# Three reorderings in a two-block transformer kernel: top-k rounds over four partition quadrants, expert pieces loaded one program sooner, feed-forward loads issued in another order

## The chip, the cores and the metric

The kernel runs on one core of a Trainium2 chip. Its time is the device time of one execution in microseconds (us), as the median of repeated runs. A core has a tensor engine (PE, with its weight loads as PEld), a vector engine (DVE), a scalar engine (ACT), GpSimd (POOL), and a sync engine (SP) whose queue issues nearly all DMAs here.

## The reference, cut to what matters

Sequence 1024, width 1024, float32. Two layers of a first block, then one second block:

```python
for l in range(DEPTH):                      # DEPTH = 2
    mod = einsum('bd,dk->bk', silu(c), w_ada[l]) + b_ada[l]     # six vectors of 1024
    h = rms_norm(x, norm1_g[l]) * (1.0 + scale1) + shift1
    ...                                     # attention and a 31 tap convolution, mixed by w_out
    x = x + gate1 * mix
    h2 = rms_norm(x, norm2_g[l]) * (1.0 + scale2) + shift2
    x = x + gate2 * expert_choice_ffn(h2, w_router[l], w_gate[l], w_up[l], w_down[l])
# expert_choice_ffn: 16 experts, each takes the 128 tokens with the largest affinity
    aff = softmax(einsum('bsd,de->bse', h, w_router))
    gate, idx = top_k(aff.transpose(0, 2, 1), 128)
    xe = h[idx]; hid = silu(xe @ w_gate) * (xe @ w_up); ye = (hid @ w_down) * gate
# second block: hgrn2 and rg-lru, then
    gate, up = split(hn @ w_gate_up); h = h + (silu(gate) * up) @ w_down
```

## The kernel before, in words

Each stage is a program of its own (an `nc.Block`): every engine has a list of instructions, they meet through semaphores, and no engine begins the next program before all have ended the last. Float32 products are made of high and low parts: ACT writes `hi`, DVE writes `lo`, and PE runs three matmuls for each product. One body of code serves both layers, so a line stands in the trace once for each.

**`conv_norm_and_mix`** ends with the w_out product. At its end SP loads rows of `w_ada` into the rows 0 to 3 of the tile `mix`; rows 4 to 7 and the weight tile `first_w` are no longer read by then. Its last instruction on DVE is the sum at L1517.

**`route`** is the next program. It (1) makes `h` (the normed tokens) and the router's logits and softmax; (2) chooses on DVE, for each of 16 experts and each half of the tokens, the 128 largest of 512 affinities: 32 rows of 512 on partitions 0 to 31, 16 rounds of `max` (the next eight values, L1720), `max_index` (their places, L1721) and `match_replace` (the eight struck out, L1722), each waiting for the one before; (3) on PE turns the eight blocks of `h` (L1774), which ACT copies to `rt_rows` (L1685) and SP stores to `h2_rows` (L1659, `h_rows` in the trace), 512 KB each; (4) on PE, between the blocks, adds up 16 products (`mod_row_step`, L1747) for the next layer's modulation. Each takes one 512 KB row of `w_ada` from a ring of four buffers `rt_ada` (SP, L1648). When all 16 are done, ACT copies the sums (L1689, semaphore `row_taken`), and PE turns them (L1788). PE's list has the wait for `row_taken` ahead of L1781 and L1782, which turn the chosen places and values back for the slot computation (L1725 to L1735 on DVE). SP also loads the first six 1 MB pieces of expert weights here (L1796), two ahead of the `rt_ada` ring and four behind its first four rows. ACT's list casts pieces 0 and 1 (L1679) ahead of the first copy of a block.

**`run_experts`** follows. Its first instruction on POOL gathers the rows of expert 0 from `h2_rows`, and PE waits for them.

**`mix_and_feed_forward`** is the last program. It runs in units: `FFT` = 22 units of gate and up, then four chunks of four units of down (units 22 to 37). A unit is seven products of PE (L3022), i = 0 to 6. SP loads a unit's raw weights with `load_raw(n)` (768 KB for unit 23 on), one of two buffers (`first_w`, `ff_raw`). Chunk 0 reads seven blocks of hidden values, 1.5 MB each, back from DRAM into slots (`load_slot`, tiles `ff_near` and `ff_rest`, L2917); `store_block` writes such blocks (L2901), `load_x` brings the rows of x back (L2922). POOL makes the sums of a unit's weights (L2996), ACT and DVE split them, and DVE does the split of unit n + 1's first sums ahead of the evacuation of unit n (L3299) that PE's product i = 4 of unit n waits for.

All loads and stores named here are in SP's one queue, in the order of SP's list.

Of the kernel before, what the change touches and what calls it, by code (L numbers as in the profile page):

```python
# [21 lines left out]
P = 128  # L22
S = 1024
# [33 lines left out]
SPLIT_EARLY = 2  # L57
N_MOD = 6
# [71 lines left out]
def build(nc, A):  # L130
# [3 lines left out]
    with ExitStack() as top:  # L134
# [397 lines left out]
        def layer(l):  # L532
            with ExitStack() as ctx:
# [8 lines left out]
                gate = (modl[:, 2, :], modl[:, 5, :])  # L542
                with ExitStack() as mixing:
                    mixing.enter_context(own_semaphores())
                    mix = sb("mix", [P, DT, S], F32, mixing)
# [22 lines left out]
                    conv_norm_and_mix(l, lc, mix, gate[0], modl)  # L568
                with own_semaphores():
                    experts_part(l, lc, modl, gain, shift[1], gate[1])  # L570
# [753 lines left out]
        def conv_norm_and_mix(l, lc, mix, gate, modl):  # L1324


            with ExitStack() as ctx:
# [11 lines left out]
                w_in = [sem(f"lo_w_in{b}") for b in range(LO_BUFS)]  # L1339

# [20 lines left out]
                with nc.Block() as block:  # L1361
                    @block.sync
                    def _(sp):
# [25 lines left out]
                        load_ada(LATE_RING + ends[1], n_steps)  # L1389

# [176 lines left out]
        def experts_part(l, lc, modl, gain, shift, gate):  # L1567
            with ExitStack() as ctx:
# [3 lines left out]
                with ExitStack() as running:  # L1572
                    raw = [sb(f"ex_raw{i}", [P, 4, HALF], F32, running)[:] for i in range(RAW - 1)]
# [17 lines left out]
        def route(l, lc, modl, gain, shift, slots, slot_gate, token, pieces):  # L1591
# [3 lines left out]
            with ExitStack() as ctx:  # L1595
# [15 lines left out]
                aff_t = sq_sum[0:2 * EXPERTS, 0:HALF]  # L1611
                best, place, place_f = (sq_sum[0:2 * EXPERTS, HALF + n * CAP:HALF + (n + 1) * CAP] for n in range(3))
                place = place.bitcast(U32)
                chosen = sb("chosen", [P, 2, 2, EXPERTS], F32, ctx)
# [13 lines left out]
                mod_bank, cols_bank, back_psum = 5, 1, psum[:, 5, 0:4 * EXPERTS]  # L1628
# [10 lines left out]
                with nc.Block() as block:  # L1639
                    @block.sync  # L1640
                    def _(sp):
# [23 lines left out]
                    def _(act):  # L1665
# [10 lines left out]
                        act.copy(aff_t, bank(0)[0:2 * EXPERTS, :]).then_inc(aff_copied, 1)  # L1676
# [15 lines left out]
                    def _(dve):  # L1692
# [2011 lines left out]
```

## Time and profile before

| | |
|---|---|
| median of 3 runs | 3468.09 us (3467.51 to 3471.37) |
| profiled execution | 3468.38 us, span 3466.6 us |
| PE busy | 3278.0 us, 95% of the span |
| DVE busy | 2723.0 us, 79% |
| DMA | 708.43 MB, mean 204 GB/s |

The profiled execution lies 0.3 us over the median. Busy time is summed over stages with different limits, so the idle stretches of PE, and what ends each, say more than the share.

### The profile page before, as it was taken

The numbers are of one execution on the slowest core, as the hardware profiler recorded it, in microseconds if no ns is written. First come the engines' busy times: TensorE is split into PE (matmuls) and PEld (weight loads), VectorE is DVE, ScalarE is ACT, GpSimd is POOL, SyncE is SP. The second block draws the span as 40 slices with busy tenths as digits, with TensorE's granted clock in tenths as the row PEclk, the third lists the DMA queues.
The fourth block names the chain that finished last, engine by engine and source line by source line (L and its number), as shares of the span: only waits on it lengthen the run. The fifth ranks groups of instructions, "written<-read, shape, count | busy, mean of one in ns | idle before, by whom it ended". The sixth has DMA issues, their size and how long they took to land. (4 is left out here: it accounts for less than half of the span.)

```text
span 3466.6 us, 43873 instructions
## 1 busy us (share of the span) xinstructions
PE 3278.0 (95%) x15396; PEld 2599.7 (75%) x15396; DVE 2723.0 (79%) x2529; ACT 1812.3 (52%) x1933; POOL 683.4 (20%) x530
## 2 busy tenths in 40 slices
PE   6999997999999899999889999999999999999898
PEld 3847973788888686597558888887877778888686
DVE  6987777898989789778789898985844498888667
ACT  5244543788888633445258888863242353344223
POOL 0202200111111020220011111103444032333232
PEclk9999998999999999999999999999999999999999
DMA  5110057999999411003689999972110334444863
GB/s 194 37 67 20 8 194 261 360 393 400 390 398 392 182 49 70 19 12 133 238 315 401 389 403 389 400 294 91 52 43 13 129 109 161 143 159 140 340 252 134
DMA packets 144682, 708.43 MB, mean 204 GB/s; under 512 B 19248, under 2 KB 27952, under 8 KB 91824
## 3 DMA queue, kind: packets, MB, share of 16 engines
q1 hardware_dynamic: 133392, 669.89, 50.4%
q0 software_dynamic: 8928, 32.51, 3.5%
q10 hardware_dynamic: 2240, 4.46, 0.3%
q8 instruction: 70, 1.15, 0.1%
q14 instruction: 52, 0.43, 0.0%
HBM read 617.14 MB, written 85.46 MB: 203 GB/s over the span
## 5 line engine op out<-in xcount | busy, mean ns | idle before, releaser
L2070 DVE TENSOR_TENSOR ex_lo<-ex_raw,ex_hi 128x2048 fp32r<-128x2048 f32 x320 | 727.4, 2290 | 114.0 <-ACT ex_hi L2004 111.3
L2004 ACT CAST ex_hi<-ex_raw 128x2048 fp32r<-128x2048 f32 x316 | 604.9, 1915 | 123.3 <-PE psum L1926 116.7
L1924 PE MATMUL psum<-ex_hi,xe_hi 128*128 128x512 f32 x1024 | 403.1, 394 | 1.3 <-DVE xe_lo L2075 1.3
L1926 PE MATMUL psum<-ex_hi,xe_lo 128*128 128x512 f32 x1024 | 400.0, 391 | 0.0
L1925 PE MATMUL psum<-ex_lo,xe_hi 128*128 128x512 f32 x1024 | 400.0, 391 | 0.0
L583 DVE SCALAR_TENSOR_TENSOR mix<-y,lcols,mix 128x1024 f32<-128x1024 f32 x186 | 274.3, 1477 | 6.0
L3022 PE MATMUL psum<-ff_rest,w_hi 128*128 128x512 f32 x776 | 241.2, 392 | 15.7 <-DVE ff_ev L3299 9.8
L1924 PEld LDWEIGHTS psum<-ex_hi,xe_hi 128*128 128x128 f32 x1024 | 193.3, 189 | 41.1 <-issue 2.0
L1926 PEld LDWEIGHTS psum<-ex_hi,xe_lo 128*128 128x128 f32 x1024 | 193.1, 189 | 40.5
L1925 PEld LDWEIGHTS psum<-ex_lo,xe_hi 128*128 128x128 f32 x1024 | 193.2, 189 | 38.9
L1924 PE MATMUL psum<-ex_hi,hid_hi 128*128 128x512 f32 x512 | 205.2, 401 | 0.0
L1926 PE MATMUL psum<-ex_hi,hid_lo 128*128 128x512 f32 x512 | 200.3, 391 | 0.0
L1925 PE MATMUL psum<-ex_lo,hid_hi 128*128 128x512 f32 x512 | 199.4, 390 | 0.0
L1873 POOL COPY idx_in<-slots 128x1 uint32 (+1 forms) x32 | 14.4, 451 | 900.5 <-PE psum L1910 516.2
L3022 PEld LDWEIGHTS psum<-ff_rest,w_hi 128*128 128x128 f32 x776 | 145.6, 189 | 49.6 <-issue 12.9
L1223 ACT ACTIVATE y<-psum,neg_max,q_scale 128x1024 f32<-128x1024 f32 x64 | 77.3, 1207 | 165.2 <-DVE neg_max L1264 165.2
L3022 PE MATMUL psum<-ff_rest,ff_a_hi 128*128 128x512 f32 x512 | 158.9, 392 | 2.8 <-DVE ff_rest L3438 1.5
L3022 PE MATMUL psum<-ff_rest,w_lo 128*128 128x512 f32 x388 | 151.8, 391 | 0.0
L2070 DVE TENSOR_TENSOR ex_lo<-first_w,ex_hi 128x2048 fp32r<-128x2048 f32 x64 | 146.5, 2288 | 3.0 <-ACT ex_hi L2004 3.0
L478 PE MATMUL psum<-h_hi,in_hi 128*128 128x512 f32 x384 | 123.1, 402 | 26.2 <-DVE h_lo L694 23.1
L2004 ACT CAST ex_hi<-first_w 128x2048 fp32r<-128x2048 f32 x64 | 121.8, 1903 | 25.7 <-PE psum L1926 25.7
L478 PE MATMUL psum<-xn_hi,w_hi 128*128 128x512 f32 x384 | 120.9, 396 | 7.2 <-DVE xn_lo L2171 6.7
(524 smaller groups left out, 7458.5 us busy)
## 6 DMA issues: line engine op xcount, KB each, us to landing
ex_raw<-w_experts_dram SPq DMA_DIRECT2D x320, 1024.0 KB, 7.3
first_w<-w_experts_dram SPq DMA_DIRECT2D x64, 1024.0 KB, 7.9
hid_rows<-x SPq DMA_DIRECT2D x71, 512.0 KB, 3.7
mix<-w_ada_dram SPq DMA_DIRECT2D x64, 512.0 KB, 4.6
first_w<-w_in_dram SPq DMA_DIRECT2D x42, 512.0 KB, 3.5
ff_rest<-hid_rows SPq DMA_DIRECT2D x13, 1536.0 KB, 14.5
rt_ada<-w_ada_dram SPq DMA_DIRECT2D x32, 512.0 KB, 7.9
ff_raw<-w_gate_up_dram SPq DMA_DIRECT2D x11, 1024.0 KB, 7.8
```

The lines of the kernel that those rows point to most:

```text
L478: mm = pe.matmul(bank(out + half), wt, xt[:, half * HALF:(half + 1) * HALF], start=first and n == 0, stop=last and n == 2)
L583: dve.scalar_tensor_tensor(out=acc, in0=y[:, j, t:t + S], scalar=lc("conv_w")[:, j * TAPS_PAD + t:j * TAPS_PAD + t + 1], in1=acc, op0=ALU. ...
L1223: act.activation(probs[:, slot, :], score_slot(slot), ACT.Exp, bias=neg_max[:, slot:slot + 1], scale=q["q_scale"][:, h, blk], accum_out=ro ...
L1873: pool.tensor_copy(idx_in[:], slots[:, bass.ds(e, 1)]).then_inc(idx_in_done, 1)
L1924: pe.matmul(bank(out), x_hi, h[:, k, :], start=first, stop=False)
L1925: pe.matmul(bank(out), x_hi, r[:, k, :], start=False, stop=False)
L1926: mm = pe.matmul(bank(out), x_lo, h[:, k, :], start=False, stop=end)
L2004: act.copy(hi[j % PARTS][:], raw[j % RAW][:]).then_inc(w_hi, 1)
L2070: dve.tensor_tensor(lo[j % PARTS][:], raw[j % RAW][:], hi[j % PARTS][:].bitcast(F32), ALU.subtract).then_inc(w_lo, 1)
L3022: mm = pe.matmul(out, wt[:, k, :], xt(k), start=fresh and k == 0 and j == 0, stop=k == kt - 1 and j == 2, skip_group_check=True)
```

## The change

1. **Rounds over quadrants.** The affinities of round r lie in the partitions of quadrant r % 4 (32 partitions each). `match_replace` reads quadrant r % 4 and writes the next one, so each quadrant keeps the state in which its eight values were found. `max_index` runs once in four rounds, over all 128 partitions, and the last `match_replace` is left out. Afterwards the values and places of the four quadrants are put in one row again: four copies of 32x32 on DVE (places), four on POOL (values).
2. **Order on PE.** L1781 and L1782 (turning the choice back) write bank 0 rather than 5, and the wait for `row_taken` stands behind the flip matmul.
3. **Three pieces sooner.** Pieces 0, 1 and 5 of the first expert (1 MB each) are loaded at the end of `conv_norm_and_mix`, into `mix` rows 4 to 7 and `first_w`; that program's SP waits until they have landed. `mix` is kept for the whole layer and serves as raw buffers 0 to 3.
4. **Feed-forward loads.** `load_raw(23)` moves behind slots 0 and 1; `load_raw(25)` moves from behind the wait for `late_out` and the loads of slots 7 and 8 to right behind `load_x(3)`.

```diff
+WITH_MIX = (0, 1, RAW - 1)
...
+                mix = sb("mix", [P, DT, S], F32, ctx)
+                raw = [mix[:, row:row + 2, :].rearrange("p a (b n) -> p (a b) n", n=HALF) for row in (HEADS, HEADS + 2, 0, 2)]
...
                         load_ada(LATE_RING + ends[1], n_steps)
+                        sp.wait_ge(lo_done, DT)
+                        sp.wait_ge(lo_split, DT)
+                        for j in WITH_MIX:
+                            load_piece(sp, early_raw[j], 0, j).then_inc(pieces_in, 16)
+                        sp.wait_ge(pieces_in, 16 * len(WITH_MIX))
...
-                        for j in range(SPLIT_EARLY):
-                            load_piece(sp, raw[j], 0, j).then_inc(loaded[j], 16)
+                        for j in WITH_MIX:
+                            sp.sem_inc(loaded[j], 16)
                         load_ada(0, NEXT_RING)
-                        for j in range(SPLIT_EARLY, RAW):
-                            load_piece(sp, raw[j], 0, j).then_inc(loaded[j], 16)
+                        for j in range(RAW):
+                            if j not in WITH_MIX:
+                                load_piece(sp, raw[j], 0, j).then_inc(loaded[j], 16)
...
                         for r in range(CAP // 8):
-                            at = slice(8 * r, 8 * r + 8)
-                            ch.step(dve.max(best[:, at], aff_t))
-                            ch.step(dve.max_index(place[:, at], best[:, at], aff_t))
-                            ch.step(dve.match_replace(aff_t, best[:, at], aff_t, -1.0))
-                        dve.tensor_copy(place_f, place).then_inc(place_done, 1)
+                            q, at = quadrant(r % 4), slice(r // 4 * 8, r // 4 * 8 + 8)
+                            ch.step(dve.max(best[q, at], states[q, :]))
+                            if r % 4 == 3:
+                                ch.step(dve.max_index(place[:, at], best[:, at], states))
+                            if r + 1 < CAP // 8:
+                                ch.step(dve.match_replace(states[quadrant((r + 1) % 4), :], best[q, at], states[q, :], -1.0))
+                        for q in range(4):
+                            dve.tensor_copy(place_row[:, in_row(q)], place[quadrant(q), :]).then_inc(place_done, 1)
...
+                    @block.gpsimd
+                    def _(pool):
+                        for q in range(4):
+                            pool.wait_ge(step, best_steps(CAP // 8 - 4 + q))
+                            pool.tensor_copy(best_row[:, in_row(q)], best[quadrant(q), :]).then_inc(best_copied, 1)
...
-                        pe.wait_ge(row_taken, 4)
-                        pe.wait_ge(place_done, 1)
+                        pe.wait_ge(place_done, 4)
+                        pe.wait_ge(best_copied, 4)
...
+                        pe.wait_ge(row_taken, 4)
                         for j in range(DT // 2):
...
                         n = FFT - 1
                         late = period_blocks(n)
-                        load_raw(n + 2)
                         stored(n_products * DOWN_CHUNKS[0] - 1)
                         for m, i in enumerate((0, 1, 2, 3, 4, 4, 5)):
                             load_slot(m, n, i)
+                            if m == 1:
+                                load_raw(n + 2)
...
                         load_x(3)
+                        load_raw(FFT + 3)
                         sp.wait_ge(late_out, 16 * LATE_BLOCKS)
                         for m in range(n_products, SLOTS):
                             load_slot(m, n, 6)
-                        for n in range(FFT + 1, n_units):
+                        for n in range(FFT + 2, n_units):
```

**SP's list where `conv_norm_and_mix` ends and `route` begins.** The line numbers are those of each kernel; `mix` from `w_ada_dram` is the last modulation row of the ending program, an `UNCONDITIONAL_BRANCH` is the change of program. Before:

```order
L1377 DMA mix<-w_ada_dram 128x1024
L1361 UNCONDITIONAL_BRANCH
L1640 UNCONDITIONAL_BRANCH
L1642 ISA
L1642 DMA w_r<-w_router_dram 128x8x16
L1796 ISA
L1796 DMA ex_raw<-w_experts_dram 128x2048
```

And now:

```order
L1384 DMA mix<-w_ada_dram 128x1024
L1832 ISA
L1832 DMA mix<-w_experts_dram 128x2048
L1832 ISA
L1832 DMA mix<-w_experts_dram 128x2048
L1832 ISA
L1832 DMA first_w<-w_experts_dram 128x2048
L1368 UNCONDITIONAL_BRANCH
L1665 UNCONDITIONAL_BRANCH
L1667 ISA
L1667 DMA w_r<-w_router_dram 128x8x16
```

Three pieces have moved ahead of the change of program, and the ring of `rt_ada` comes first in `route`.

**SP's list in the feed-forward, from the raw weights of unit 22 (`first_w`) on.** `ff_raw` from `w_down_dram` is unit 23 at first and unit 25 the second time; `ff_near` and `ff_rest` from `hid_rows` are slots, `x` from `x_rows` is `load_x`. Before:

```order
L2896 DMA ff_raw<-w_down_dram 128x1536
L2917 DMA ff_near<-hid_rows 128x3072 x2
L2917 DMA ff_rest<-hid_rows 128x3072 x5
L2901 DMA hid_rows<-x 128x1024 x3
L2896 DMA first_w<-w_down_dram 128x1536
L2901 DMA hid_rows<-ff_near 128x1024 x2
L2922 DMA x<-x_rows 128x2x1024
L2901 DMA hid_rows<-ff_rest 128x1024 x4
L2922 DMA x<-x_rows 128x2x1024 x2
L2917 DMA ff_rest<-hid_rows 128x3072
L2917 DMA ff_near<-hid_rows 128x2048
L2917 DMA ff_rest<-hid_rows 128x1024
```

And now:

```order
L2953 DMA ff_near<-hid_rows 128x3072 x2
L2932 DMA ff_raw<-w_down_dram 128x1536
L2953 DMA ff_rest<-hid_rows 128x3072 x5
...
L2958 DMA x<-x_rows 128x2x1024 x2
L2932 DMA ff_raw<-w_down_dram 128x1536
L2953 DMA ff_rest<-hid_rows 128x3072
L2953 DMA ff_near<-hid_rows 128x2048
L2953 DMA ff_rest<-hid_rows 128x1024
```

Unit 23's weights went behind two slots, and unit 25's (before, the row after the twelve shown) ahead of the last three slot loads.

## Rows read from the trace of the kernel before

**Rows 1.** The page: busy us, share and instructions of each engine.

```profile
PE 3278.0 (95%) x15396; PEld 2599.7 (75%) x15396; DVE 2723.0 (79%) x2529; ACT 1812.3 (52%) x1933; POOL 683.4 (20%) x530
```

**Rows 2.** Waits of layer 1's `route`, 545 to 616 us: total, times, longest.

```profile
PE psum L1747 <- DMA rt_ada<-w_ada_dram: 10.5, 5, 7.0
...
PE psum L1781 <- ACT rt_ada L1689: 3.4, 1, 3.4
```

**Rows 3.** DVE in order of time: start, us, line, tiles, idle before.

```profile
564.33 0.68 DVE L1720 MAX8 sq_sum<-sq_sum 32x8 f32<-32x512 f32 x1 [1.31 <-ACT sq_sum L1676]
565.05 0.08 DVE L1721 MATCH_VALUE_LOAD sq_sum<-sq_sum 32x8 f32 x1
...
565.83 0.08 DVE L1722 MATCH_VALUE_LOAD sq_sum<-sq_sum 32x8 f32 x1
...
566.61 0.68 DVE L1720 MAX8 sq_sum<-sq_sum 32x8 f32<-32x512 f32 x1
...
600.75 0.21 DVE L1723 CAST sq_sum<-sq_sum 32x128 f32<-32x128 uint32 x1
...
605.25 0.17 DVE L1737 TENSOR_TENSOR mod<-psum,b_ada 128x16 f32<-128x16 f32 x1
```

**Rows 4.** PE in order of time, the products of the modulation.

```profile
574.43 3.58 PE L1747 MATMUL psum<-rt_ada,c_act 128*1 128x512 f32 x8 [7.04 <-DMA rt_ada<-w_ada_dram]
...
597.17 1.03 PE L1747 MATMUL psum<-rt_ada,c_act 128*1 128x512 f32 x4 [0.24 <-DMA rt_ada<-w_ada_dram]
```

**Rows 5.** ACT in order of time, the first two block copies and `row_taken`.

```profile
567.81 1.90 ACT L1685 COPY rt_rows<-psum 128x1024 f32<-128x1024 f32 x2
...
600.16 2.37 ACT L1689 COPY rt_ada<-psum 1x512 f32<-1x512 f32 x4
```

**Rows 6.** Windows of `route`: busy by engine, then TensorE clock, DMA share, GB/s.

```profile
550.00:574.00 24.00, 15.86 (x72) 4.92 (x72) 18.41 (x35) 15.22 (x15) 0.00 (x0) 0.86 1.01 406
574.00:597.00 23.00, 19.30 (x84) 6.73 (x84) 21.93 (x53) 5.06 (x5) 0.00 (x0) 0.82 0.94 347
```

**Rows 7.** SP's last issue in `conv_norm_and_mix` of layer 1.

```profile
534.53 0.33 SPq L1377 DMA_DIRECT2D mix<-w_ada_dram  x1
```

**Rows 8.** DVE's last instruction in that program.

```profile
546.18 0.18 DVE L1517 TENSOR_TENSOR modl<-psum,b_ada 128x24 f32<-128x24 f32 x1 [4.47 <-PE psum L217]
```

**Rows 9.** Waits of PE in the feed-forward, 3180 to 3300 us.

```profile
PE psum L3022 <- DVE ff_ev L3299: 9.1, 2, 7.2
...
PE psum L3022 <- DMA ff_rest<-hid_rows: 5.5, 4, 2.4
```

**Rows 10.** SP's issues in the feed-forward.

```profile
3204.03 0.33 SPq L2896 DMA_DIRECT2D ff_raw<-w_down_dram  x1
...
3242.80 1.40 SPq L2922 DMA_DIRECT2D x<-x_rows  x2
3251.74 0.33 SPq L2917 DMA_DIRECT2D ff_rest<-hid_rows  x1
...
3253.06 0.43 SPq L2896 DMA_DIRECT2D ff_raw<-w_down_dram  x1
```

**Rows 11.** PE in the feed-forward: product 1 of unit 21, products of units 24, 25.

```profile
3200.81 0.62 PE L3022 MATMUL psum<-ff_near,ff_a_hi 128*128 128x512 f32 x2
...
3269.94 1.19 PE L3022 MATMUL psum<-ff_rest,w_hi 128*128 128x512 f32 x2 [7.24 <-DVE ff_ev L3299]
...
3278.80 0.61 PE L3022 MATMUL psum<-ff_near,w_hi 128*128 128x512 f32 x2
```

**Rows 12.** POOL: the first sums of unit 25.

```profile
3266.12 0.99 POOL L2996 TENSOR_TENSOR ff_s<-ff_raw 128x384 f32<-128x384 f32 x1 [12.53 <-DMA ff_raw<-w_down_dram]
```

**Rows 13.** DVE: the last weight split of unit 23.

```profile
3239.12 0.96 DVE L3289 TENSOR_TENSOR w_lo<-ff_raw,w_hi 128x768 fp32r<-128x768 f32 x1 [0.23 <-ACT w_hi L3087]
```

**Rows 14.** Windows of the feed-forward, columns as in rows 6.

```profile
3206.00:3264.00 58.00, 49.36 (x212) 39.04 (x210) 35.34 (x50) 14.98 (x25) 11.99 (x10) 1.00 1.01 417
3268.00:3274.00 6.00, 4.06 (x10) 3.22 (x11) 4.33 (x7) 1.24 (x2) 1.77 (x3) 0.50 0.01 3
```

More of the change, by code:

```diff
@@ L542, in layer @@
                 gate = (modl[:, 2, :], modl[:, 5, :])
+                mix = sb("mix", [P, DT, S], F32, ctx)
+                assert CT == HEADS == 4
+                raw = [mix[:, row:row + 2, :].rearrange("p a (b n) -> p (a b) n", n=HALF) for row in (HEADS, HEADS + 2, 0, 2)]
                 with ExitStack() as mixing:
                     mixing.enter_context(own_semaphores())
-                    mix = sb("mix", [P, DT, S], F32, mixing)
                     with ExitStack() as before:
@@ L567, in layer @@
                         attend(l, lc, y, mix, q)
-                    conv_norm_and_mix(l, lc, mix, gate[0], modl)
+                    conv_norm_and_mix(l, lc, mix, gate[0], modl, raw)
                 with own_semaphores():
-                    experts_part(l, lc, modl, gain, shift[1], gate[1])
+                    experts_part(l, lc, modl, gain, shift[1], gate[1], raw)
         def conv_taps(dve, lc, y, mix, step, done):
@@ L1322, in _, with conv_norm_and_mix @@
                                                      op0=ALU.mult, op1=ALU.add).then_inc(centred, 1)
-        def conv_norm_and_mix(l, lc, mix, gate, modl):
+        def conv_norm_and_mix(l, lc, mix, gate, modl, pieces_raw):
             with ExitStack() as ctx:
@@ L1339, in conv_norm_and_mix @@
                 w_in = [sem(f"lo_w_in{b}") for b in range(LO_BUFS)]
+                pieces_in = sem("lo_pieces_in")
+                load_piece = expert_pieces(l)
+                early_raw = {j: pieces_raw[j] for j in WITH_MIX[:-1]}
+                early_raw[RAW - 1] = first_w[:].rearrange("p b k m -> p (b k m)").rearrange("p (a n) -> p a n", n=HALF)
                 def raw_of(n):
@@ L1565, in _, with experts_part @@
                         inverse_norms(act, r, sum_bank, sq_sum)
-        def experts_part(l, lc, modl, gain, shift, gate):
+        def experts_part(l, lc, modl, gain, shift, gate, raw):
             with ExitStack() as ctx:
@@ L1572, in experts_part @@
                 with ExitStack() as running:
-                    raw = [sb(f"ex_raw{i}", [P, 4, HALF], F32, running)[:] for i in range(RAW - 1)]
+                    raw = raw + [sb(f"ex_raw{i}", [P, 4, HALF], F32, running)[:] for i in range(len(raw), RAW - 1)]
                     raw.append(first_w[:].rearrange("p b k m -> p (b k m)").rearrange("p (a n) -> p a n", n=HALF))
@@ L1610, in route, with quadrant, in_row, best_steps @@
                 halves = sb("rt_halves", [P, TB // 2, 2, EXPERTS], F32, ctx)
-                aff_t = sq_sum[0:2 * EXPERTS, 0:HALF]
-                best, place, place_f = (sq_sum[0:2 * EXPERTS, HALF + n * CAP:HALF + (n + 1) * CAP] for n in range(3))
-                place = place.bitcast(U32)
+                def quadrant(q):
+                    return slice(q * 2 * EXPERTS, (q + 1) * 2 * EXPERTS)
+                assert 4 * 2 * EXPERTS == P
+                states = sq_sum[:, 0:HALF]
+                per_quadrant = CAP // 4
+                best, place = (sq_sum[:, HALF + n * per_quadrant:HALF + (n + 1) * per_quadrant] for n in range(2))
+                place = place.bitcast(U32)
+                best_row, place_row = (sq_sum[quadrant(0), HALF + n * CAP:HALF + (n + 1) * CAP] for n in range(1, 3))
+                best_copied = sem("rt_best_copied")
+                def in_row(q):
+                    return slice(q * per_quadrant, (q + 1) * per_quadrant)
+                def best_steps(r):
+                    return 2 * r + r // 4 + 1
                 chosen = sb("chosen", [P, 2, 2, EXPERTS], F32, ctx)
@@ L1626, in route @@
                     "ada_used", "mod_row_taken", "mod_turned", "mod_done")]
-                mod_bank, cols_bank, back_psum = 5, 1, psum[:, 5, 0:4 * EXPERTS]
+                mod_bank, cols_bank, back_psum = 5, 1, psum[:, 0, 0:4 * EXPERTS]
                 flip_psum = psum[:, 4, 0:4 * EXPERTS].rearrange("p (a b e) -> p a b e", a=2, b=2)
@@ L1675, in _ @@
                         act.wait_ge(aff_turned, 1)
-                        act.copy(aff_t, bank(0)[0:2 * EXPERTS, :]).then_inc(aff_copied, 1)
+                        act.copy(states[quadrant(0), :], bank(0)[0:2 * EXPERTS, :]).then_inc(aff_copied, 1)
                         for j in range(SPLIT_EARLY):
```

4 lines of the change are left out of this document (2 added, 2 removed).

## The prediction

> **What bounds the kernel now.** I read the page first: TensorE (PE) is busy 95% of the span [rows 1], so time can come only from the stretches in which it stands idle or runs slowly. The list of waits, taken stage by stage, gives two such places that the change touches.
>
> The first is `route`, once in each layer. PE waits 10.5 us there for rows of `rt_ada`, and 3.4 us for the copies behind `row_taken` [rows 2]. Three chains run side by side. (a) DVE's choice of tokens goes from 564.33 to 600.96 [rows 3]. (b) The modulation: the last row of `rt_ada` lets PE go on at 597.17 [rows 4], ACT's four copies run from 600.16 to 602.53 [rows 5], and only then does PE turn the choice back, because the wait stands ahead of it. (c) The DMA queue, which feeds (b): its share is 1.01 at 406 GB/s from 550 to 574 and 0.94 at 347 GB/s from 574 to 597 [rows 6]. So the stage is bound by transfers, and the choice ends only 1.6 us before `row_taken`. The program ends with DVE's sum at 605.42 [rows 3]. The reader should see that no single chain can be shortened for much: DVE and the transfers lie within 2 us of each other.
>
> The second is the start of the down products. There PE waits 5.5 us for slots and 9.1 us for DVE's L3299 [rows 9]. The long one ends at 3269.94 after 7.24 us [rows 11]. What is late is the raw weights of unit 25: POOL got them at 3266.12 after idling 12.53 us [rows 12], and they were issued last, at 3253.06 [rows 10], into a queue that moves 417 GB/s at a share of 1.01 for 58 us [rows 14].
>
> **The feed-forward loads.** One queue in list order reproduces the old landings, so I cost the new list the same way.
>
> *Front of the queue.* Before, it starts with unit 23's raw weights at 3204.03 [rows 10]. Now slot 0 is first. It needs product 0 of unit 21, and product 1 begins at 3200.81 [rows 11]; adding 0.2 us for the last matmul to drain, slot 0 is issued at 3201.0. Its 1.57 MB last 3.8 us at 417 GB/s, so slot 1 (issued one product of 2.7 us later) and the raw weights join without a gap. The same bytes begin 3.0 us sooner, and everything behind them lands 3.0 us sooner. PE's 5.5 us of slot waits [rows 9] shrink to 2.5. The stores and `load_x` behind them shift too, so the 1.9 us wait that is left of the 9.1 keeps its size and comes 3.0 sooner. Unit 23's raw weights now land about 4.5 us later than before (3.8 + 3.8 more bytes ahead, 3.0 sooner); POOL's use of them has no DMA wait before, and several products pass before PE needs the result, so I cost this at nothing; without that cover it would be up to 4 us.
>
> *Unit 25's raw weights.* They move ahead of slots 7 and 8, which are 3.1 MB, or 7.5 us at 417 GB/s. The condition of their own, the split of unit 23, ends at 3240.08 [rows 13], before the x loads of 3242.80 [rows 10]. Landing: 3266.1 - 7.5 - 3.0 = 3255.6. From landing to PE going on took 3269.94 - 3266.12 = 3.8 us, so 3259.4. PE itself arrives at 3269.94 - 7.24 - 3.0 = 3259.7. The wait of 7.24 us is gone, within 1 us. Slots 7 and 8 now land 1.9 us (0.79 MB) behind that, near 3263; they are needed only two units, some 20 us, later.
>
> *The clock.* After that wait TensorE was granted 0.50 of full speed, its lower level of 1.2 GHz, from 3268 to 3274, where it had 1.00 (2.4 GHz) before [rows 14]. The 27 matmuls from 3269.94 to 3278.80 took 8.86 us [rows 11]; at full speed a pair starts every 0.45 us, 6.1 us in all. Without the idle stretch there is no drop: 2.7 us.
>
> Sum: 3.0 + 7.24 + 2.7 = **12.9 us**. Afterwards PE is never short of a slot in the old trace, so the gain stays. Bounds: 11 (a remainder of 1 us, and the clock still dips) to 13.5.
>
> **The choice on DVE.** A round is 2.28 us: `max` 0.72, `max_index` 0.78, `match_replace` 0.78, from the starts 564.33, 565.05, 565.83, 566.61 [rows 3]. Now there are 16 `max`, 15 `match_replace` and 4 `max_index`: 11.5 + 11.7 + 3.1 = 26.3 us, ending at 590.7. No row shows these operations over 128 partitions or across quadrants. The nearest row is the operation itself, 512 elements on each of 32 partitions in 0.68 us, which is 1.3 ns an element with all 32 side by side. Below, a price of 0.78 for 128 partitions; above, four times that, 9.4 us more per layer, which would put the end at 600.9 again and leave `route` 1.5 us of gain. I take the lower, since the partitions already run side by side. Four 32x32 copies instead of one cost at most 4 x 0.21 = 0.8. End: 591.5 instead of 600.96. POOL's four copies wait for earlier steps only and lie beside DVE's last `max_index`; at most 1 us. Lower bound of this part nothing, upper bound 9.5.
>
> A rule that speaks against it: successive rows show no overlap to lose, since each step is waited for and the value load's 0.08 us already stands whole before its partner [rows 3]. The Trainium skill (VectorE: DVE Perf Modes, "Two Vector instructions with no wait between them") says that an instruction whose output starts in another quadrant than the last output is held until all earlier ones have finished; every new `match_replace` is such a one. By the row the choice ends at 591.5; by the rule, if each replace lost another 0.08 us, at 592.7, an estimate. Neither is the last chain below.
>
> **The transfers of `route`.** Three pieces, 3.15 MB, leave its queue: at 406 GB/s 7.7 us. So rows 4 and 5 of the ring, before there near 574.3 [rows 4], land near 566.6. But the next store cannot be issued sooner: block 0's copy starts at 567.81 behind two casts of ACT [rows 5], and rows 6 and 7 stand behind that store in SP's list. With some 2 us from issue to data (an estimate: unit 23's weights were issued at 3204.03 [rows 10], and the queue is full from 3206 [rows 14]) the queue runs dry until about 570.3, and 3.7 of the 7.7 us are given back. From there 10 rows and 5 stores of 0.52 MB follow up to the last row: 7.9 MB at 347 GB/s [rows 6] are 22.7 us, so 593.0 instead of 597.17. Bounds: at 406 GB/s 589.8; with the worst mix, 594.5.
>
> Then 5.36 us to the end of ACT's copies, as before (602.53 - 597.17): 598.4. In the new order only PE's four turns (about 1.1 us) and DVE's sum (0.17) follow, 1.4 us: 599.8. The slots' own chain starts when PE has turned block 7, near 595, and needs about 3 us: 598. So the program ends at 599.8 rather than 605.42, **5.6 us** sooner, of which 4.2 are the transfers and 1.4 the order on PE. Both layers: **11.2 us** (7 to 17).
>
> **The pieces in `conv_norm_and_mix`.** SP's last issue there ends at 534.86 [rows 7], so the three start at 534.9 to 535.7. Before them half a MB is under way; 3.15 MB at 417 GB/s are 7.6 us: landed by 545.5. DVE's last instruction ends at 546.36 [rows 8]. It is hidden behind the norm and the last modulation, by 0.9 us. If the cover were gone, each us late costs one us per layer.
>
> **Sum.** 12.9 + 11.2 = 24.1. Against the profiled execution 3468.4 - 24.1 = 3444.3; it lies 0.3 over the median, so 3444.0 is my number.
>
> **Rivals.**
> 1. *The shorter queue gives nothing in `route`.* The seven us are lost to the ring of four buffers: each row waits for a buffer, each block copy for a store. Then only the order on PE helps, 1.4 us per layer: 3468.1 - 12.9 - 2.8 = 3452.4. For it speaks that the new queue runs dry for 4 us; against it that the share is 0.94 or more afterwards [rows 6], so bytes decide.
> 2. *The transfers of `route` run at the faster rate.* At 406 GB/s the last row lands at 589.8, and the program ends at 596.6, 8.8 us sooner: 3437.6.
> 3. *Unit 25's weights still come late*, because x and the stores ahead of them are the mass in the queue. Only the 3.0 us in front stay: 3468.1 - 3.0 - 11.2 = 3453.9. My sum leaves 0.3 us of margin, so a part of this is possible; the whole needs the load to land 7 us later than the bytes say.
> 4. *Slower.* The `match_replace` that crosses quadrants costs more than the one in place, and the choice becomes the last chain. From its end the turn back, the slots and the sum need about 3 us. To lose the 12.9 us of the feed-forward as well, `route` must end 6.5 us later than before, at 611.9, so DVE at 608.9, 17.4 us after my 591.5: 1.2 us more for each of 15 replaces, 1.8 us instead of 0.66. Beyond that the kernel is slower; at 2.3 us each it ends at 619, 13.7 later per layer, 3468.1 - 12.9 + 27.4 = 3482.6. No row points that way; only the rule on held instructions does, and by far less.
>
> **How the numbers follow.** Chances: my forecast 0.70, rival 1 0.11, rival 2 0.08, rival 3 0.07, rival 4 0.04 (half of it beyond the point where it decides). My forecast's own range is 11 to 13.5 plus 7 to 17, 3437.6 to 3450.1. Rivals 1 and 3 lie at 3452 and 3454; the range takes in rival 2 and most of rival 1: 3435 to 3453. About 0.2% (7 us) is what a measurement can tell from no change: faster 0.94, same 0.04, slower 0.02.
>
> **What would show it.** In the new trace: 16, 4 and 15 operations in 26.3 us; L1781's successor no longer ended by ACT's copy; PE's first long wait for `rt_ada` (7.0 us) gone, a short one near 569 to 572 in its place; `route` 5.6 us shorter in each layer; the program before it not longer than now. In the feed-forward: slot waits of 2.5 us, no 7 us wait, no stretch at 0.50 behind it. The prediction is wrong if SP's wait for the pieces ends the ending program, if the last row of `rt_ada` lands after 595, or if unit 25's weights land after 3257.

## The result, and the profile after

The changed kernel takes 3443.9 us (median of 4 runs, 3441.5 to 3450.1) against 3467.9 us before (4 runs, 3467.5 to 3471.4). The ratio is 0.9931 with a 95% interval of 0.9918 to 0.9944: 24 us faster, as forecast. A second set of 5 runs, made later, gave 3441.6 us beside 3469.4 for the kernel before, and 0.9918 (0.9905 to 0.9932): 27.7 us. The forecast of 24.1 us lies inside both intervals.

The profiled execution took 3450.1 us, 6 us more than its own median. What is known of those 6 us is told under the experiments.

The page after. Its first part gives busy time and share of each engine, to be held against [rows 1].

```profile
span 3447.2 us, 43845 instructions
## 1 busy us (share of the span) xinstructions
PE 3278.2 (95%) x15396; PEld 2600.2 (75%) x15396; DVE 2705.2 (78%) x2483; ACT 1814.0 (53%) x1933; POOL 685.9 (20%) x538
```

PE's busy time is the same in a shorter span: in this pair of profiles the gain is idle time. Matmuls also count as busy for longer where the clock is low, so what the clock gave back in one place and took in another can't be read from this sum.

**The choice.** DVE's timeline of the changed kernel in layer 1: first rounds, last round (start us, duration, engine, line, operation, out<-in).

```profile
564.33 0.68 DVE L1746 MAX8 sq_sum<-sq_sum 32x8 f32<-32x512 f32 x1 [1.31 <-ACT sq_sum L1702]
565.04 0.08 DVE L1750 MATCH_VALUE_LOAD sq_sum<-sq_sum 32x8 f32 x1
565.13 0.67 DVE L1750 MATCH_REPLACE8 sq_sum<-sq_sum 32x512 f32<-32x512 f32 x1
565.84 0.68 DVE L1746 MAX8 sq_sum<-sq_sum 32x8 f32<-32x512 f32 x1
...
569.61 0.09 DVE L1748 MATCH_VALUE_LOAD sq_sum<-sq_sum 128x8 f32 x1
569.72 0.70 DVE L1748 FIND_INDEX8 sq_sum<-sq_sum 128x8 uint32<-128x512 f32 x1
570.45 0.08 DVE L1750 MATCH_VALUE_LOAD sq_sum<-sq_sum 32x8 f32 x1
...
591.16 0.77 DVE L1752 CAST sq_sum<-sq_sum 32x32 f32<-32x32 uint32 x4
594.97 0.23 DVE L1754 COPY chosen<-psum 128x64 f32<-128x64 f32 x1 [3.03 <-PE psum L1817]
```

It starts at 564.33, as in [rows 3], and its last copy ends at 591.93 (forecast 591.5, before 600.96). A replace into the next quadrant takes 0.80 us from start to start (565.04 to 565.84), where the one in place took 0.78 [rows 3]; a search over 128 partitions takes 0.84 (569.61 to 570.45), where one over 32 took 0.78. DVE then waits 3.03 us for PE: the choice is no longer the last chain.

**The transfers of `route`.** PE's timeline in the same stage.

```profile
567.32 1.88 PE L1782 MATMUL psum<-rt_ada,c_act 128*1 128x512 f32 x8
...
574.45 1.87 PE L1782 MATMUL psum<-rt_ada,c_act 128*1 128x512 f32 x4 [4.22 <-DMA rt_ada<-w_ada_dram]
...
592.64 1.03 PE L1782 MATMUL psum<-rt_ada,c_act 128*1 128x512 f32 x4 [0.23 <-DMA rt_ada<-w_ada_dram]
...
594.62 0.24 PE L1816 MATMUL psum<-const,sq_sum 32*128 32x32 f32 x1
...
595.25 0.43 PE L1820 MATMUL psum<-chosen,flip 128*128 128x64 f32 x2 [0.32 <-DVE chosen L1754]
598.07 0.66 PE L1824 MATMUL psum<-const,rt_ada 128*128 128x128 f32 x4 [2.39 <-ACT rt_ada L1715]
```

The ring's rows 4 and 5 are there when PE asks (567.32, no wait; before, 7.0 us [rows 4]). The next pair is late by 4.22 us. The prediction had a short wait near 569 to 572 in this place; the real one is longer, ends at 574.45, and PE runs slowly behind it (four matmuls in 1.87 us, where eight took 1.88 at 567.32). The last step is at 592.64 (forecast 593.0, before 597.17 [rows 4]), and PE turns the choice back at once, ahead of the wait for ACT. Only that wait of 2.39 us and DVE's sum at 598.94 (before 605.25) stand behind.

Stretches of the changed kernel (from:to, length, then busy us and count of PE, PEld, DVE, ACT, POOL, then PEclk, DMA share, GB/s).

```profile
566.00:571.00 5.00, 4.23 (x26) 1.99 (x24) 4.75 (x11) 3.71 (x4) 0.00 (x0) 1.00 0.41 147
571.00:574.00 3.00, 0.00 (x0) 0.00 (x0) 2.83 (x7) 1.01 (x1) 0.00 (x0) 0.69 0.99 244
574.00:593.00 19.00, 15.44 (x70) 4.98 (x72) 16.92 (x39) 4.05 (x4) 0.81 (x4) 0.87 0.99 381
```

The queue is dry from 566 to 571 (147 GB/s), as the prediction worked out: SP issues the next two rows behind the first store. That this order makes the hole is shown under 5.

```profile
562.20 1.19 SPq L1673 DMA_DIRECT2D rt_ada<-w_ada_dram  x2
568.83 0.33 SPq L1685 DMA_DIRECT2D h_rows<-rt_rows  x1
569.36 1.11 SPq L1673 DMA_DIRECT2D rt_ada<-w_ada_dram  x2
```

**The feed-forward.** PE's waits there (times 8.0 us earlier than before, for what was gained upstream).

```profile
3218.91 0.70 PE L3060 MATMUL psum<-ff_rest,w_hi 128*128 128x512 f32 x2 [1.44 <-issue]
3224.04 0.70 PE L3060 MATMUL psum<-ff_rest,w_hi 128*128 128x512 f32 x2 [0.78 <-DMA ff_rest<-hid_rows]
...
3237.22 0.71 PE L3060 MATMUL psum<-ff_rest,w_hi 128*128 128x512 f32 x2 [2.72 <-DVE ff_ev L3337]
```

At the place of the four slot waits of 5.5 us [rows 9] stand 0.78 us and a gap of 1.44 us for which the view names no releaser ("issue"), 2.2 together (forecast 2.5). The 7.24 us [rows 11] are gone, and a wait of 2.72 us (forecast 1.9) is what is left of DVE's L3299. POOL gets unit 25's raw weights early enough:

```profile
3247.70 1.01 POOL L3034 TENSOR_TENSOR ff_s<-ff_raw 128x384 f32<-128x384 f32 x1 [6.04 <-DMA ff_raw<-w_down_dram]
```

That is 3255.7 on the old time scale, where the forecast was 3255.6 and the old row 3266.12 [rows 12].

### The profile page after: what moved, and what is told of

The parts are those of the page before. It is cut to its first block and busy times, and to the rows that moved or that the text cites. A ratio compares the mean times of both kernels' runs of the same rounds, so it can differ in the third digit from the quotient of the medians.

```text
span 3447.2 us, 43845 instructions
## 1 busy us (share of the span) xinstructions
PE 3278.2 (95%) x15396; PEld 2600.2 (75%) x15396; DVE 2705.2 (78%) x2483; ACT 1814.0 (53%) x1933; POOL 685.9 (20%) x538
## 5 line engine op out<-in xcount | busy, mean ns | idle before, releaser
L2106 DVE TENSOR_TENSOR ex_lo<-mix,ex_hi 128x2048 fp32r<-128x2048 f32 x256 | 583.3, 2291 | 44.7 <-ACT ex_hi L2040 42.2
L2040 ACT CAST ex_hi<-mix 128x2048 fp32r<-128x2048 f32 x252 | 481.8, 1913 | 104.1 <-PE psum L1962 101.1
L2106 DVE TENSOR_TENSOR ex_lo<-ex_raw,ex_hi 128x2048 fp32r<-128x2048 f32 x64 | 146.7, 2292 | 69.7 <-ACT ex_hi L2040 69.5
L2040 ACT CAST ex_hi<-ex_raw 128x2048 fp32r<-128x2048 f32 x64 | 122.3, 1911 | 16.5 <-PE psum L1962 16.5
```

The costliest lines, as they stand in the source:

```text
L2040: act.copy(hi[j % PARTS][:], raw[j % RAW][:]).then_inc(w_hi, 1)
L2106: dve.tensor_tensor(lo[j % PARTS][:], raw[j % RAW][:], hi[j % PARTS][:].bitcast(F32), ALU.subtract).then_inc(w_lo, 1)
```

## The experiments

Two stretches are read off each profile, since a whole span varies by several us: from the first `max` of the choice to PE's first turn of gathered rows `xe` ("route"), and from that turn in layer 2 to the end of the span ("rest", with the feed-forward in it). For the changed kernel in layer 1 that is 564.33 to 607.20, 42.87 us.

The kernels were timed in groups, each beside the kernel before. Its median was 3467.9 us in the first group (both first profiles), 3469.5 beside the kernels of experiments 1 and 2, 3468.6 beside those of 4 and 5, and 3469.4 beside those of 3 and 6 and the second "ring ahead". Differences below are taken within a group. Each is uncertain by 3 to 5 us, as its interval says; the stretches of one and the same code vary by 1 to 3 us from profile to profile.

| kernel | median us | ratio to before (95%) | route 1 | route 2 | rest |
|---|---|---|---|---|---|
| before, first profile | 3467.9 | | 49.28 | 48.53 | 1699.5 |
| before, second profile | 3468.8 | 0.9999 (0.9990 to 1.0008) | 48.24 | 48.62 | 1700.4 |
| changed, first profile | 3443.9 | 0.9931 (0.9918 to 0.9944) | 42.87 | 43.50 | 1689.1 |
| changed, second profile | 3441.6 | 0.9918 (0.9905 to 0.9932) | 42.18 | 41.49 | 1686.8 |
| feed-forward only | 3456.7 | 0.9963 (0.9950 to 0.9977) | 48.02 | 48.45 | 1688.0 |
| route only | 3459.2 | 0.9970 (0.9957 to 0.9982) | 42.19 | 42.11 | 1700.7 |
| quadrants only | 3466.5 | 0.9989 (0.9980 to 0.9998) | 45.73 | 47.29 | 1701.2 |
| early pieces only | 3469.5 | 1.0000 (0.9991 to 1.0009) | 47.86 | 47.45 | 1701.2 |
| unit 25 only | 3459.9 | 0.9974 (0.9964 to 0.9985) | 47.93 | 48.64 | 1690.4 |
| slots first only | 3465.9 | 0.9991 (0.9982 to 1.0000) | 48.26 | 48.65 | 1696.7 |
| search each round | 3456.7 | 0.9963 (0.9950 to 0.9977) | 48.55 | 48.33 | 1688.1 |
| ring first | 3443.6 | 0.9918 (0.9905 to 0.9932) | 42.65 | 40.90 | 1688.3 |
| ring ahead, first | 3443.8 | 0.9924 (0.9910 to 0.9937) | 42.13 | 42.24 | 1686.4 |
| ring ahead, second | 3437.3 | 0.9902 (0.9887 to 0.9917) | 41.93 | 41.55 | 1687.0 |

**1. The two halves apart.** One kernel is the one before with only the feed-forward's list changed; the other is the changed kernel without that:

```diff
...
-                        load_raw(n + 2)
                         stored(n_products * DOWN_CHUNKS[0] - 1)
                         for m, i in enumerate((0, 1, 2, 3, 4, 4, 5)):
                             load_slot(m, n, i)
+                            if m == 1:
+                                load_raw(n + 2)
...
                         load_x(3)
+                        load_raw(FFT + 3)
                         sp.wait_ge(late_out, 16 * LATE_BLOCKS)
...
```

> The kernel before with only the two moves in the feed-forward's load list (slots 0 and 1 ahead of unit 23's raw weights; unit 25's raw weights ahead of slots 7 and 8). My theory: all terms of the feed-forward, 12.9 us by the prediction; the trace of the changed kernel suggests 11 to 11.5, because a wait of 2.7 us and a stretch at the lower clock remain: 3455 to 3457 us. Rival (unit 25's weights stay late): 3 us, 3465. Rival (the feed-forward and the route change share a gain, so that alone each is worth more or less): anything outside 10 to 14 us.

> The changed kernel with the feed-forward's load list of before: quadrants, early pieces and the order on PE only. My theory: 11.2 us less than before (6.3 and 4.7 in the two layers of the changed trace), 3456 to 3458, and it and the run with the feed-forward alone add up to the whole 24 us. Rival (the shorter queue gives nothing, only the order on PE): 2.8 us, 3465.

Measured: 3456.7 us, 12.9 less than the 3469.5 of before beside it, and 3459.2 us, 10.3 less. The sum is 23.2 us, against 24 and 27.7 for both together in the two sets, so the halves add up as far as the intervals can tell (8 to 17 us for the feed-forward, 6 to 15 for `route`). Rivals 1 and 3 of the prediction (2.8 us from route, 3.0 from the feed-forward) are out.

**2. The two parts of the route change apart.** Early pieces out of the changed kernel, and the feed-forward's change too (the list of SP as it was). What stays is the choice in quadrants and the new order on PE; below it is called quadrants only:

```diff
...
-                        for j in WITH_MIX:
-                            sp.sem_inc(loaded[j], 16)
+                        for j in range(SPLIT_EARLY):
+                            load_piece(sp, raw[j], 0, j).then_inc(loaded[j], 16)
                         load_ada(0, NEXT_RING)
...
```

> The kernel before with the choice in quadrants and the new order on PE, but all expert pieces loaded in route as before. My theory: the stage is bound by transfers, the last row of rt_ada stays at 597.2 in the first layer, so only the order on PE helps: 1.4 us a layer, 3465.0. DVE ends its choice near 592 and then waits. Rival (the choice was the bound): 5 us or more a layer, 3458 or less.

and early pieces alone, with the choice and PE's order of before:

```diff
...
+                        for j in WITH_MIX:
+                            load_piece(sp, early_raw[j], 0, j).then_inc(pieces_in, 16)
+                        sp.wait_ge(pieces_in, 16 * len(WITH_MIX))
...
```

> The kernel before with three pieces loaded one program sooner, the choice in one quadrant and PE's old order kept. My theory: the last row of rt_ada moves from 597.2 to about 593 in the first layer, ACT's copies end near 598.4, but DVE's choice still ends at 601.0 and is waited for: the program ends about 1.5 us sooner a layer, 3465. Rival (transfers alone carry the gain): 4.2 us a layer, 3459.5.

Measured: 3466.5 us for quadrants only (3.0 less; 0.2 to 2.0 per mille), and no difference for the pieces only (within 0.9 per mille, 3 us, either way). Together they bring 10.3. PE's timeline with quadrants only:

```profile
596.75 1.03 PE L1772 MATMUL psum<-rt_ada,c_act 128*1 128x512 f32 x4 [0.23 <-DMA rt_ada<-w_ada_dram]
...
598.74 0.24 PE L1806 MATMUL psum<-const,sq_sum 32*128 32x32 f32 x1
```

and with early pieces only:

```profile
590.59 1.03 PE L1760 MATMUL psum<-rt_ada,c_act 128*1 128x512 f32 x4 [0.23 <-DMA rt_ada<-w_ada_dram]
591.55 1.10 PE L1787 MATMUL psum<-const,rt_h 128*128 128x128 f32 x8
600.38 0.28 PE L1794 MATMUL psum<-const,sq_sum 32*128 32x32 f32 x1 [7.74 <-DVE sq_sum L1736]
```

In the first, the last row of `rt_ada` is as late as without the change (31.1 us behind the first `max`, where five profiles with the old code have 30.0 to 32.8) and the choice stands ready; DVE waits 5.76 us. In the second, the last row comes 4 us sooner in the stage (27.0 us behind the first `max` at 563.60, against 31.1 behind that at 565.70), and PE waits 7.74 us for the choice. Each part alone opens a wait on the other. I expected 3 us of the pieces; the two stages show 0.4 and 1.2 us (47.86 and 47.45 against 48.24 and 48.62), so that expectation was too high by the stages. The interval of the time excludes neither those 1.6 us nor the 3.

**3. What a search costs.** The changed kernel with a search in every round, which keeps only the walk round the quadrants:

```diff
...
-                            if r % 4 == 3:
-                                ch.step(dve.max_index(place[:, at], best[:, at], states))
+                            ch.step(dve.max_index(place[:, at], best[:, at], states))
...
```

> The changed kernel with an index search over 128 partitions in every round (16, not 4), so that only the walk round the quadrants is kept. A search costs 0.84 us between starts in the changed trace, so DVE's choice takes 12 x 0.84 = 10.1 us more and ends near 602.0 in layer 1, 7.4 us behind the turn of block 7. Theory: PE then waits for the choice, the program ends about 7 us later (less than 10.1 by the 2.7 us that DVE now waits): both layers 13 to 14 us, 3458. Rival (DVE's choice has more slack than 3 us): under 10 us.

Measured: 3456.7 us, 15.1 more than the changed kernel on the same chip; the stages are 6.4 and 6.8 us longer. The theory (13 to 14 us) is right; of the 10.1 us more on DVE, 3.3 to 3.7 find slack. DVE at the end of the choice, in its timeline:

```profile
599.62 0.70 DVE L1747 FIND_INDEX8 sq_sum<-sq_sum 128x8 uint32<-128x512 f32 x1
600.35 0.78 DVE L1751 CAST sq_sum<-sq_sum 32x32 f32<-32x32 uint32 x4
```

PE's timeline at the same time:

```profile
591.49 1.10 PE L1808 MATMUL psum<-const,rt_h 128*128 128x128 f32 x8
601.18 0.31 PE L1815 MATMUL psum<-const,sq_sum 32*128 32x32 f32 x1 [8.59 <-DVE sq_sum L1751]
```

With the searches back, the choice ends near its old time and the stage has its old length, although the transfers are early. It is the 12 saved searches that count, not the quadrants as such. This kernel also has the new order on PE, and its time is that of the feed-forward change alone (3456.7 us both): with a choice of the old length, the early pieces and the order on PE together bring nothing that can be told. Whether the order on PE alone, in the kernel before, is worth anything was not run.

**4. The two moves of the feed-forward apart.**

```diff
...
                         load_x(3)
+                        load_raw(FFT + 3)
                         sp.wait_ge(late_out, 16 * LATE_BLOCKS)
...
```

> The kernel before with only unit 25's raw weights moved ahead of slots 7 and 8. By the prediction's terms: the 7.24 us wait goes, 2.7 us of the lower clock with it, the 3.0 us in front stay lost: 9.9 us less, 3459.5 where before is 3469.5. Rival (the clock does not come back, because another short wait lets it fall): 7 to 8 us. Rival (both moves are needed for either gain): under 4 us.

and, alone, slots 0 and 1 ahead of `load_raw(n + 2)` (the first lines of the diff under 1).

> The kernel before with only slots 0 and 1 moved ahead of unit 23's raw weights. By the prediction's term: everything in the queue 3.0 us sooner, slot waits of PE 2.5 instead of 5.5 us, the long wait of 7.24 us for unit 25 keeps its size: 3.0 us less, 3466.5 where before is 3469.5. Rival (unit 23's weights, now later, hold POOL and then PE up): 0 or slower, and POOL's first sum of unit 23 shows a DMA wait.

Measured: 3459.9 us (8.7 less) and 3465.9 us (2.7 less); by the stretch "rest", against the mean of 1700.6 of the five profiles with the old list, 10.2 and 3.9 less. PE's long waits with unit 25 only:

```profile
3234.92 1.19 PE L3023 MATMUL psum<-ff_rest,w_hi 128*128 128x512 f32 x2 [2.85 <-DMA ff_rest<-hid_rows]
3248.51 0.70 PE L3023 MATMUL psum<-ff_rest,w_hi 128*128 128x512 f32 x2 [0.23 <-DVE ff_ev L3300]
```

and with the slots first only:

```profile
3232.05 0.70 PE L3023 MATMUL psum<-ff_rest,w_hi 128*128 128x512 f32 x2 [2.39 <-DMA ff_rest<-hid_rows]
3245.75 1.19 PE L3023 MATMUL psum<-ff_rest,w_hi 128*128 128x512 f32 x2 [3.24 <-DVE ff_ev L3300]
3267.49 1.19 PE L3023 MATMUL psum<-ff_rest,w_hi 128*128 128x512 f32 x2 [4.36 <-DVE ff_ev L3300]
```

In the first the wait for unit 25 is gone and the slot waits stay; in the second the slots come sooner and the long wait stays, though at 4.36 us and not 7.24, which I had not expected: the wait before it is longer, PE runs slowly behind that one (1.19 us for two matmuls, where 0.70 is usual) and so comes later to the next (3.24 + 4.36 = 7.6, where 1.8 + 7.2 = 9.1 was). That is not the doing of the slots: the profile with early pieces only, whose feed-forward list is the old one, has 2.97 and 4.43 us in these two places. POOL's first sum of unit 23 shows no DMA wait there. The two moves add up within the noise (11.4 us by the times, 14.1 by the stretch, 12.9 for both), and the weights of unit 25 are the larger part by far. The interval of the slots alone (0.9982 to 1.0000) just reaches no gain; the stretch and the shorter slot waits speak for it.

**5. The dry queue.** Is the time from 566 to 571 to be had? One swap in SP's list in `route`:

```diff
...
-                        load_ada(NEXT_RING, NEXT_RING + 2)
+                        load_ada(NEXT_RING, NEXT_RING + 4)
                         for t in range(TB):
...
-                            load_ada(min(NEXT_RING + 2 + 2 * t, 2 * DT), min(NEXT_RING + 4 + 2 * t, 2 * DT))
+                            if t:
+                                load_ada(min(NEXT_RING + 2 + 2 * t, 2 * DT), min(NEXT_RING + 4 + 2 * t, 2 * DT))
```

> The changed kernel with one swap in SP's list in route: rows 6 and 7 of rt_ada are issued ahead of the first block's store, not behind it. My theory of the dry queue: in the changed trace the queue moves 147 GB/s from 566 to 571 because these rows wait behind ACT's copy of block 0 (issued 569.36, although PE was done with their buffers near 566.4). The swap gives back about 3 us a layer: PE's wait of 4.2 us shrinks to 1.2, the last row lands near 589.7, the choice then ends (591.9) behind it, program end near 596. 6 us less than the changed kernel: 3438. Rival (the ring's buffers and the row copies give the time back further on): PE's first wait shrinks, but a wait of the same size appears at blocks 4 to 6, and the time stays at 3444.

In the other kernel the loop's `load_ada` reads `NEXT_RING + 4 + 2 * t` and `NEXT_RING + 6 + 2 * t` for every t.

> The changed kernel with SP's list in route shifted by a whole group: rows 6 and 7 ahead of store 0, rows 8 and 9 behind store 0, and so on, two rows further ahead of the stores throughout. Theory: the same first gain as with the single swap, but each store now stands behind a wait for buffers that PE frees one block later, so the copies of ACT that wait for stores come later; between the single swap (3438) and the changed kernel (3444). Rival (the queue never runs dry and this is the best of the three): below 3437.

Measured: 3443.6 and 3443.8 us, which can't be told from the changed kernel. The stretches with the single swap (columns as above):

```profile
566.00:571.00 5.00, 5.00 (x28) 1.75 (x28) 4.75 (x10) 5.00 (x4) 0.00 (x0) 1.00 0.91 342
574.00:593.00 19.00, 12.82 (x58) 4.53 (x56) 17.96 (x40) 4.86 (x5) 0.81 (x4) 0.82 0.99 359
549.00:593.00 44.00, 33.73 (x156) 11.33 (x156) 37.26 (x73) 21.10 (x20) 0.81 (x4) 0.84 0.96 345
```

PE's waits for the rows in its timeline:

```profile
578.10 3.58 PE L1783 MATMUL psum<-rt_ada,c_act 128*1 128x512 f32 x8 [3.53 <-DMA rt_ada<-w_ada_dram]
...
592.06 1.03 PE L1783 MATMUL psum<-rt_ada,c_act 128*1 128x512 f32 x4 [2.65 <-DMA rt_ada<-w_ada_dram]
593.34 1.03 PE L1783 MATMUL psum<-rt_ada,c_act 128*1 128x512 f32 x4 [0.26 <-DMA rt_ada<-w_ada_dram]
```

The hole is filled (342 GB/s in place of 147), and the wait of 4.22 us comes back at the next pair, 3.53 us, and again at the end, 2.65 us. Over the whole stretch the queue moves 345 GB/s in place of 337, but the changed kernel itself has 346 in its second profile. The last step is 27.5 us behind the first `max` (593.34 - 565.82), where the changed kernel has 28.3 and, in its second profile, 27.6. My theory of 3 us a layer is wrong, and the time is the rival's, 3444. Why the queue is slower afterwards (359 GB/s after 574 in place of 381), for the buffers of the ring or for the stores among the loads, no run separates.

> The changed kernel with rows of rt_ada issued a group further ahead of the stores, a second time, now beside the changed kernel on the same chip. Theory: no gain that can be told (within 2 us of it), since the first wait for rows only moved two blocks back. Rival: 3 us or more faster, as the first profile's span (3442.0 to 3447.2) would have it.

Measured: 3437.3 us beside 3441.6 for the changed kernel. Its ratio, 0.9902 (0.9887 to 0.9917), overlaps that of the changed kernel, 0.9918 (0.9905 to 0.9932), and the stages are as long. Whether it is faster stays open; the two runs of it say 0 and 4 us.

**6. What an execution varies by.** Both kernels as they are, once more.

> The changed kernel, unaltered, profiled and timed a second time. Question: from the start of the experts of layer 1 to the choice of layer 2 the same instructions took 1107.4 to 1107.9 us in three profiles and 1104.9 to 1105.8 us in seven others; the difference is the granted clock at two idle places of the attention. Theory (the clock's dips come and go from execution to execution): this stretch can come out at 1105 to 1106 here, and the span then is 2 us shorter than the 3447.2 of the first profile. Rival (the shorter route shifts something that makes the dips): again 1107.4 or more. Median near 3444 in either case.

> The kernel before, unaltered, profiled a second time: the same question from its side. From the first max of the choice to the first gathered rows on PE it took 49.3 us in layer 1 in the first profile, where four kernels with the same code there took 47.9 to 48.3. Theory (execution to execution): near 48.1, which puts the gain of the route change in layer 1 at 5.6 us and not 6.4. Rival: again 49.3. Median near 3469, ratio 1.

The stretch between the two layers' stages (from the first turn of `xe` in layer 1 to the first `max` of layer 2) took 1104.7 us this time, with the same code and the same shorter route that had 1107.4 (607.20 to 1714.63) in the first profile, and the span was 3438.9 us, not 3447.2. In the first profile of the changed kernel (from:to, length, PE busy, PEclk, DMA share, GB/s):

```profile
1429.70:1432.20 2.50, 1.16 (x9) 1.00 0.00 0
1432.20:1434.70 2.50, 2.50 (x8) 0.52 0.17 39
1434.70:1437.20 2.50, 2.50 (x17) 0.80 0.09 20
```

and at the same place of the kernel before, each a little behind an idle time of PE of 2.59 us (it waits for DVE's `y` until 1431.04 and 1437.56):

```profile
1436.11:1438.61 2.50, 1.05 (x9) 1.00 0.00 0
1438.61:1441.11 2.50, 2.50 (x14) 1.00 0.17 39
1441.11:1443.61 2.50, 2.50 (x24) 1.00 0.09 20
```

After the same wait the granted clock falls to 0.52 in one execution and stays at 1.00 in another. At a second place, where PE waits 4.1 us for DVE until 1593.81, the low clock lasts longer too, and the two places make most of the 2.7 us between these profiles. So part of the 6 us by which the first profiled execution stood over its median are such dips. They are not tied to the new `route`: the profile with unit 25 only, whose `route` is the old one, falls to 0.69 and 0.63 behind the same wait. But three of the six profiles with the short route have the long stretch (1107.4 to 1107.9 us) and none of the eight others (1104.8 to 1105.8), so that the change makes them more frequent is not excluded. The kernel before gave 48.24 us for the stage of layer 1 at its second profile, as its kin did (47.9 to 48.3), so 49.28 was a high one.

## Why the prediction was right

*Feed-forward, 12.9 us.* Measured 12.9 with that change alone (8 to 17 by its interval), and 12.9 by the stretch "rest" (1700.6 over five profiles with the old list, 1687.7 over seven with the new). That both agree to 0.1 us is partly luck. Its terms: 3.0 in front, 2.7 by the time alone and 3.9 by the stretch; 7.24 + 2.7 for unit 25 and the clock, together 9.9, 8.7 by the time and 10.2 by the stretch. Two smaller things were off, both to the same side: the wait that stays is 2.7 us, not 1.9, and behind it the clock still dips, which I had forecast away:

```profile
3238.00:3240.00 2.00, 2.00 (x6) 0.50 1.03 422
3240.00:3242.00 2.00, 2.00 (x7) 0.66 1.02 414
3242.00:3244.00 2.00, 2.00 (x11) 1.00 1.04 429
```

Both tell in the first pair of profiles. From POOL's sum of unit 21 (L3003, 3192.61) to that of unit 26 (3289.40) the first profile before took 96.8 us, the first after (L3041, 3184.64 to 3269.96) 85.3: 11.5 us, not 12.9. What made up for them is nothing that the prediction had: the other four profiles with the old list took 97.2 to 98.5 us, with more slot waits or more of the low clock, so the profile that I read was the shortest of five; the other six with the new list took 83.6 to 85.5. The means differ by 12.7 us.

The landing by bytes at 417 GB/s was within 0.1 us for unit 25. Slots 7 and 8 were forecast for 3263, which is 7.5 us behind it; the "1.9 us" of the prediction is by how much they come later than without this move, not the distance. The later landing of unit 23's weights cost nothing, as said.

*Route, 5.6 us a layer.* Between the second profiles: 6.1 and 7.1 us; between all profiles with the old code there (five) and the new (three), 5.9 and 6.2. The time with the route change alone says 10.3 for both layers (6 to 15 by its interval), the forecast was 11.2. For the term of the order on PE (1.4 us a layer) speaks the quadrants-only kernel, 3.0 us for both layers (0.7 to 6.9) where 2.8 was expected; but it has the shorter choice too, and with the old length of the choice the order brought nothing (3 above), so the 1.4 us belong to the two together. The term of the transfers (4.2) is borne out in its size: 597.17 to 592.64 is 4.5, and over all these profiles the last row comes 3.6 us sooner behind the first `max` in layer 1 and 4.7 in layer 2. Its two parts were a little off and cancel: from 571 the queue moves 362 GB/s up to 593, where 347 from 570.3 on was forecast. And it counts only with the choice out of the way: by itself it is worth nothing that can be told. The prediction said that DVE and the transfers lie within 2 us of each other; that is why.

*The choice, 26.3 us.* It took 26.8 (564.33 to 591.16) and the copies 0.77 where 0.8 was said. The lower price for 128 partitions was the right one: 0.84 us, not four times 0.78. The 0.5 us are 4 x 0.06 for the wider searches and 15 x 0.02 for the replaces that cross. Those 0.02 us are at most what shows here of the rule in the Trainium skill (VectorE: DVE Perf Modes, "Two Vector instructions with no wait between them") that an instruction whose output starts in another quadrant is held: here each step waits for the one before anyway. That they come from this rule no run shows. Rival 4 needed 1.2 us a replace.

*The pieces in `conv_norm_and_mix`.* Hidden, as forecast: the next program's first issue of SP stands at 547.68 in the changed kernel and 547.66 before, and in layer 2 it comes 1.5 us behind DVE's last sum in both.

*The dry queue.* Its place and its cause were right, 570.3 forecast for the restart, and the stretch up to 571 is the slow one. The 3.7 us that the prediction charged to it were not its cost: with the hole filled the last row came 0.2 us sooner behind the first `max` in layer 1 and 1.5 in layer 2 (against the mean of the changed kernel's two profiles and the one with the route change alone), and the queue was slower afterwards (359 GB/s in place of 381). The last row came where it was forecast, but a fixed rate behind the hole is not what sets it, and what does stays open.

*Rival 2* (the faster rate, 406 GB/s) did not come: the stretch after 574 has 381, with stores among the loads, and the last row came at 592.64, not 589.8.

## What to carry to other kernels

Where two chains end within 2 us of each other, cost the edit of each alone and both together: here they were worth 3, 0 and 10 us. A search over 128 partitions costs almost what one over 32 does, so work in independent partition groups can be gathered into one instruction. Where a queue is full and works in list order, count bytes and rate to see when an item lands: moving late weights ahead of slots that are needed two units later took away the whole wait here. Filling a short hole ahead of a full queue can be worth next to nothing. And a forecast read from one profile carries that profile's luck: here about 1 us in the feed-forward and 1 us in the first stage of `route`.

## What was not expected of the hardware

The granted clock behind one and the same idle time of 2.59 us stayed at 1.00 in ten of the fourteen profiles and fell in the other four (the changed kernel's first, route only, ring first, unit 25 only), to between 0.52 and 0.63 over 2.5 us, of kernels with the same code there. With a second such place it moves a span by 2 to 3 us, and with it a single pair of profiles: read a stretch in several before a difference of that size is believed. Replaces of 32 x 512 elements whose output lies in another quadrant cost 0.80 us in place of 0.78.
